# A float32 decoder trunk on one core: gate and up weights land in four slots instead of six

## The reference

```
u = rmsnorm(h, pre_ffn_g[i])
ff = (jax.nn.silu(u @ w_gate[i]) * (u @ w_up[i])) @ w_down[i]
h = h + rmsnorm(ff, post_ffn_g[i])
```

## Time and profile before

| | |
|---|---|
| median of three runs | 1069.28 us (1069.28 to 1069.93) |
| the profiled execution's own time | 1069.55 us |
| its span (first to last instruction) | 1067.8 us |
| PE busy | 1058.0 us, 99% |
| DVE busy | 912.6 us, 85% |
| ACT busy | 608.2 us, 57% |
| POOL busy | 75.6 us, 7% |
| moved by DMA | 208.05 MB, mean 195 GB/s |

### The profile page before, as it was taken

The page is one execution under the profiler, slowest core; times in us unless marked ns, Lnnn a source line. Parts: engine busy times, 40 slices in busy tenths (PEclk is TensorE's granted clock), DMA queues, the critical chain, the costliest instruction groups (busy, mean ns, idle before and its releaser), DMA issues. The chain is left out here.

```text
span 1067.8 us, 15447 instructions
## 1 busy us (share of the span) xinstructions
PE 1058.0 (99%) x5704; PEld 916.7 (86%) x5704; DVE 912.6 (85%) x1115; ACT 608.2 (57%) x754; POOL 75.6 (7%) x67
## 2 busy tenths in 40 slices
PE   9999999999999999999999999999999999999997
PEld 8999999999888888888888888888888888888885
DVE  5699987646556779999999999999999899988887
ACT  6554455746545576566556665665665555655553
POOL 6000101101000001001011011010000000000000
PEclk9999999999999999999999999999999999999999
DMA  8655535444386476666666666566666665666665
GB/s 272 212 175 171 165 112 158 139 139 139 119 294 218 140 266 226 217 198 188 206 203 210 195 199 218 180 200 190 193 201 219 219 203 192 196 213 213 205 200 195
DMA packets 113208, 208.05 MB, mean 195 GB/s; under 512 B 9184, under 2 KB 46496, under 8 KB 111856
## 3 DMA queue, kind: packets, MB, share of 16 engines
q1 hardware_dynamic: 111952, 201.49, 58.8%
q10 hardware_dynamic: 608, 4.20, 1.0%
q0 software_dynamic: 576, 1.40, 0.4%
HBM read 202.86 MB, written 4.19 MB: 194 GB/s over the span
## 5 line engine op out<-in xcount | busy, mean ns | idle before, releaser
L630 ACT ACTIVATE w_hi<-raw 128x1024 fp32r<-128x1024 f32 x279 | 291.8, 1058 | 182.3 <-PE ps L1798 83.6
L993 DVE TENSOR_TENSOR w_lo<-raw,w_hi 128x1024 fp32r<-128x1024 f32 x266 | 322.8, 1228 | 70.7 <-ACT w_hi L630 70.4
L1796 PE MATMUL ps<-w_hi,uf 128*128 128x512 f32 x470 | 183.5, 390 | 0.1
L1798 PE MATMUL ps<-w_hi,uf 128*128 128x512 f32 x470 | 182.9, 389 | 0.0
L1797 PE MATMUL ps<-w_lo,uf 128*128 128x512 f32 x470 | 182.8, 389 | 0.0
L1467 PE MATMUL ps<-u,w_hi 128*128 128x272 f32 (+1 forms) x544 | 158.8, 292 | 0.0
L911 ACT CAST t_hi<-tx 128x1024 fp32r<-128x1024 f32 x110 | 114.2, 1051 | 77.8 <-DVE tx L1287 66.5
L1469 PE MATMUL ps<-u,w_hi 128*128 128x272 f32 (+1 forms) x544 | 155.9, 287 | 0.0
L1470 PE MATMUL ps<-u,w_lo 128*128 128x272 f32 (+1 forms) x544 | 155.7, 286 | 0.0
L1299 DVE TENSOR_TENSOR t_lo<-tx,t_hi 128x1024 fp32r<-128x1024 f32 x110 | 130.4, 1227 | 0.0
L1796 PEld LDWEIGHTS ps<-w_hi,uf 128*128 128x128 f32 x470 | 88.2, 188 | 18.7 <-issue 0.5
(11 more groups left out here) (286 smaller groups left out, 1726.7 us busy)
## 6 DMA issues: line engine op xcount, KB each, us to landing
raw<-in_w_down SPq DMA_DIRECT2D x88, 512.0 KB, 4.1
raw<-in_w_in SPq DMA_DIRECT2D x72, 512.0 KB, 3.8
raw<-in_w_gate SPq DMA_DIRECT2D x132, 256.0 KB, 3.0
raw<-in_w_up SPq DMA_DIRECT2D x132, 256.0 KB, 3.5
raw<-in_w_out SPq DMA_DIRECT2D x32, 512.0 KB, 4.2
raw_x<-in_w_gate SPq DMA_DIRECT2D x44, 256.0 KB, 3.0
raw_x<-in_w_up SPq DMA_DIRECT2D x44, 256.0 KB, 3.9
arena<-in_x SPq DMA_DIRECT2D x2, 1024.0 KB, 6.2
```

The source lines that it names most:

```text
L630: act.activation(w_hi[:, slot, :], raw_of(q), ACT.Copy).then_inc(hi_done, 1)
L993: dve.tensor_tensor(w_lo[:, slot, :], raw_of(q), hi_view(w_hi[:, slot, :]), ALU.subtract).then_inc(lo_done, 1)
L1796: pe.matmul(o, a[0], b[0], start=start, stop=False)
L1798: return pe.matmul(o, a[1], b[0], start=False, stop=stop)
```

## The change

`raw_x` is given up. In blocks 1 to 8, too, a chunk lands in one of four slots, in turn, as in blocks 0 and 9 to 12. Nothing is added or left out on PE, DVE, ACT or POOL: each has the same instructions in the same order, reading `raw` where it read `raw_x`. The number and the order of the loads stay too. What differs is the slot of each load, and the chunk whose split SP waits for before it.

```diff
@@ -128,7 +128,7 @@
     SUM_AT = {4: 11, 10: 12, 12: 13, 18: 14, 22: 15, 24: 16, 28: 17, 32: 18, 36: 19}
     SUM_NO = {d: i for i, d in enumerate(SUM_AT.values())}
     F_SUM_AT = {10: 0, 12: 1, 13: 2, 14: 3}
-    WITH_SPARE, WITH_SLOTS = range(1, 10), range(1, 9)
+    WITH_SPARE = range(1, 10)
     ROUND = ["PPPPPPPP"] + ["PZPZPZZP" if g in WITH_SPARE else "PPZPZPZP" for g in range(1, NFG)] + ["PPPPZPPZPPZPPZPZPZPZPP", "PPPZPZPZPZPZPZPZPZPZPP"]
     BEGIN = [Q_FFN + KT * g for g in range(NFG)] + [Q_DOWN + FT * n for n in range(DW)]
     END = Q_DOWN + DW * FT
@@ -171,16 +171,11 @@
 
         return max((y for y in range(z) if buffers_of(y) == buffers_of(z)), default=None)
 
-    RSLOTS = WSLOTS + 2
     RAW_AT, RAW_BEFORE, RAW_COUNT = {}, {}, {}
     last_in = {r: Q_FFN - WSLOTS + r for r in range(WSLOTS)}
-    counts = {r: 16 * (Q_FFN // WSLOTS) if r < WSLOTS else 0 for r in range(RSLOTS)}
+    counts = {r: 16 * (Q_FFN // WSLOTS) for r in range(WSLOTS)}
     for q in range(Q_FFN, END):
-        if q % 2 == 0:
-            last_in.update({r: last_in.get(r, -1) for r in range(WSLOTS, RSLOTS)})
-            roomy = place_of(q)[0] in WITH_SLOTS
-            at = min(range(0, RSLOTS if roomy else WSLOTS, 2), key=lambda r: last_in[r])
-        r = at + q % 2
+        r = q % WSLOTS
         counts[r] += 32 if place_of(q)[0] < NFG else 16
         RAW_AT[q], RAW_BEFORE[q], RAW_COUNT[q] = r, last_in[r], counts[r]
         last_in[r] = q
@@ -231,15 +226,12 @@
         t_lo2 = sb_at("t_lo2", [P, 4, DCOLS], F32R, a_spare)
         t_hi2 = sb_at("t_hi2", [P, 4, DCOLS], F32R, a_spare + 16 * DCOLS)
         sums_of, hi_of, lo_of = (tx, tx2), (t_hi, t_hi2), (t_lo, t_lo2)
-        raw_x = sb_at("raw_x", [P, 2, CE], F32, a_inner + 4 * 4 * max(WITH_SLOTS) * 2 * SEQ)
 
         def raw_of(q):
-            r = raw_at(q)
-            return raw[:, r, :] if r < WSLOTS else raw_x[:, r - WSLOTS, :]
+            return raw[:, raw_at(q), :]
 
         def raw_pair(q):
-            r = raw_at(q)
-            return raw[:, r:r + 2, :] if r < WSLOTS else raw_x[:, :, :]
+            return raw[:, raw_at(q):raw_at(q) + 2, :]
         rows_u = tx[:, 0, :].rearrange("p (k t) -> p k t", k=2)
         sums_w = tx[:, 1, :].rearrange("p (s t) -> p s t", s=4)
         xs = sb_at("xs", [P, NQ, D], F32, a_xt)
@@ -365,7 +357,7 @@
             return ctx.enter_context(nc.semaphore(name))
 
         slot_free = sem("slot_free")
-        raw_landed = [sem(f"raw_landed{s}") for s in range(RSLOTS)]
+        raw_landed = [sem(f"raw_landed{s}") for s in range(WSLOTS)]
         hi_done, lo_done, chunks_used = sem("hi_done"), sem("lo_done"), sem("chunks_used")
         x_landed = [sem(f"x_landed{m}") for m in range(3)]
         grow_landed, vec_landed, sw_landed, gbc_landed, stored = (
@@ -492,9 +484,7 @@
                     for m in range(NQ):
                         sp_eng.dma_start(out_v[:, m, :], h2rows[:, m, :]).then_inc(h2_kept, 16)
                 r, p = RAW_AT[q], RAW_BEFORE[q]
-                if p < 0:
-                    sp_eng.wait_ge(h2_sq, NQ)
-                elif p in POOL_NO:
+                if p in POOL_NO:
                     sp_eng.wait_ge(lo_pool, POOL_NO[p] + 1)
                 else:
                     sp_eng.wait_ge(lo_done, lo_by_dve(p))
```

## The result

The changed kernel takes 1074.17 us (median of 6 runs, 1073.08 to 1076.18), the kernel before 1069.29 us in 6 runs beside it. The ratio is 1.0046, interval 1.0036 to 1.0056: slower by 4.9 us. The profiled execution took 1074.35 us with a span of 1072.6 us at a mean granted clock of 0.998, as before.

A forecast was written before the change was run, and what follows sets the result against it. PE was taken as the bound. Entry 0.7 + block 1 0.47 - 0.5 given back + 7 x 0.67 = 5.4 us, 5.2 at PE, counted down to 5.0: 1074.3 us, range 1071.0 to 1077.8.

The forecast's parts named there:

- PE is the bound: Blocks 8 and 9: PE busy 41.70 of 41.70 us; DVE's split ends 0.22 us before PE's chunk 4 weight load.
- First wait: DVE's sums of chunks 10-11, blocks 1 to 9: load's way 4.93 us against DVE's 4.46, 0.47 us late.
- Second wait: DVE's sums of chunks 2-3 at the fold: load's way 4.88 us against DVE's 4.68, 0.2 us late.
- Not given back at the fold: DVE's 0.87 us of room per block at the fold is already spent; the 0.47 us delay goes on in full.
- Entry: Block 1: chunk 3's load lands at 412.84, so the sums of chunks 2-3 begin 0.7 us late.
- Seven rounds: Blocks 2 to 9: seven times 0.67 us adds 4.7 us to DVE's lateness by block 9's sums.
- The sum: Whole kernel: DVE 5.4 us late, PE 5.2 us, counted down to 5.0 us, giving 1074.3 us.
- PE's waits: At chunk 4 of blocks 2 to 9, PE gains waits on DVE's split of some 0.6 us each.
- the ring: DVE and the loads wait on each other in turn, a round taking 0.67 us a block more than PE's; chance 0.74.
- Rival 3: Slower: POOL's split blocking DVE's sums in block 1, or slow loads, make it 1077 to 1080 us; chance 0.13.
- the way of the load: From a split through SP's issue and the landing to the next sums: 4.93 us at chunks 10-11, 4.88 at 2-3.
- rival 2: Delay given back at every fold, chunk 3's load fitting into 4.68 us: 1069.5 us, no measurable change; chance 0.11.

The follow-up runs named there:

- the other profiled execution: The changed kernel run again unaltered, in a later series on one chip: 1073.29 us (5 runs), ratio 1.0032 against the kernel before.
- later-issue kernel: Against the changed kernel, chunk 3's load in blocks 1 to 9 also waits for DVE's split of its own block's chunk 0: 1076.22 us, ratio 1.006.

## Why the prediction was right

- **PE is the bound, and DVE stands 0.22 us behind it.** Right. PE is late by 4.85 us at chunk 4 of block 9, DVE's sums of the same block by 749.74 - 744.71 = 5.03: 0.2 us of room between them, as forecast.
- **First wait, chunks 10-11, 0.47 us.** Right as a mean, too large for this execution. From the split of chunk 7 to the sums, the changed kernel takes 4.51 to 4.94 us in blocks 1 to 8, 4.77 in the mean, where DVE's own way is 4.46: 0.31 us. The 4.93 us of the earlier trace rows was at the slow end of this scatter. In the other profiled execution the mean is 4.98, so 0.52 us, a load that took 5.7 us to land in block 2 among them.
- **Second wait, chunks 2-3, 0.2 us.** Mis-sized the other way. 4.64 to 5.74 us in blocks 2 to 9, 4.99 in the mean, against 4.68: 0.31 us, and 0.30 in the other execution. Together 0.62 a block by the trace, and 0.60 by the distance of neighbouring blocks (42.31 us, forecast 42.4), where 0.67 was forecast; the other execution has 0.80.
- **Not given back at the fold.** Right, and shown: where chunk 3's load doesn't hang on chunk 15, it is given back (1069.96 us).
- **Entry.** Too large. Block 2's sums of chunks 2-3 stand 453.60 - 452.76 = 0.84 us later, of which 0.65 was there before block 1: 0.19, where 0.67 was forecast (0.48 in the other execution). The load in block 1 cost 0.27 (413.09 against 412.17 + 0.65) rather than 0.7, and the idle time before the first fold fell from 1.04 to 0.29 us.
- **Seven rounds.** 5.03 - 0.84 = 4.19 us, forecast 4.7; 5.6 in the other execution.
- **The sum.** 4.2 us at PE from the slots, forecast 5.0, and 0.65 us that the argument knew nothing of and that belongs to this execution's beginning. So the hit on this execution (1074.35, forecast 1074.6) is in part luck. The other one began 0.28 us early and lost 5.8 us to the slots. The forecast 5.0 is the middle of the two, and the medians of the two series, 4.9 and 3.7 us above the kernel before, show how wide a single number scatters: the size is right to about 1 us, not to tenths.
- **PE's waits, some 0.6 us in each block.** Right in the mean, wrong in the detail. PE's delay grows by 0.9, 0.8, 0.2, 1.5, 0.1, 0.2 and 0.5 us in blocks 3 to 9 and not in block 2, and to see it one has to look at the weight loads. The 1.5 us come from the load that took 5.1 us to land in block 6: a late landing stays in the ring. The landings scatter by 1 us and more, and the changed kernel's runs scatter over 3 to 4 us where those of the kernel before do over 0.7 to 1.4.
- **Rival 3, the collision in block 1.** Didn't happen in the changed kernel; 1 us later it does, as the later-issue kernel shows.

The step that was argued badly is the way of the load. It was taken as a constant of 4.9 us from the split. What the runs show is a load that takes 2.9 to 3.7 us when it is issued late enough, and that otherwise lands some 2.3 us behind the 512 KB of the chunk issued 1.1 us before it. For the forecast this did no harm, since the rows that it used for the two waits were loads with such a predecessor; the prediction touched on it only in rival 2 ("issued some 1.1 us behind chunk 2's"). For the first expectation of the later issue, 1083 us, it did.

## What to carry to other kernels

To price a buffer that is given up, compare two ways between the same two points: the work of the waiting engine from the release of the slot to its next use, and the release, issue and landing of the load behind its predecessor; some 0.3 us too little, twice per round, was worth 0.4 to 0.5% here. Then ask whether the lateness enters the next load: a ring with no idle time left passes it on in full, and two small waits cost more together than apart. Before paying with memory, see whether the consumer waits for more than its next instruction needs: one wait moved two instructions down did as much as the third pair of slots.

## What the runs showed of the hardware

- Of two 512 KB loads issued 1.1 us apart on one queue, the second landed 4.0 to 5.1 us after its issue, spaced 1.2 us further 2.9 to 3.7, and with half of the first one's bytes left out 3.2 to 4.3. The landing time of a load is no property of the load alone.
- DVE and POOL: a two-input pass of 0.68 us took 1.29, 2.88 or 2.89 us when POOL's split ran, as a longer instruction, with no idle time in brackets. DVE's busy time contains this waiting: it fell from 912.6 to 908.4 us although the work is the same. The sums of chunks 2-3 in blocks 2 to 9, 1.29 us before and 0.69 after, give 8 x 0.60 = 4.8 us of it; they came later and met POOL no more.
- A wait of PE of up to 0.6 us shows as 0.2 or not at all in the matmuls' records. Those of the weight loads show it, but say too much: between 405 and 800 us their waits add up to 6.3 us in the changed kernel, and PE's products fell back by 4.1 (8.3 and 5.8 in its other execution). The loss itself is read from when the same product starts.
- Landings of one and the same load scatter from block to block: chunk 3's second transfer took 4.0 to 5.1 us in blocks 2 to 9 of one execution, chunk 11's once 5.7 where 4.0 to 4.8 was usual.
